# Routing in a two-layer expert model: token rows turned in half tiles, and late modulation blocks placed between other TensorE work

## What is computed

```
mod = silu(c) @ w_ada[l] + b_ada[l]            # shift1, scale1, gate1, shift2, scale2, gate2
h   = rms_norm(x, p['norm2']) * (1.0 + scale2) + shift2
x   = x + gate2 * expert_choice_ffn(h, ...)

def expert_choice_ffn(h, w_router, w1, w3, w2):
    cap = CAPACITY_FACTOR * n_tok // N_EXPERTS       # 64 latent, 16 context tokens each
    aff = jax.nn.softmax((xt @ w_router), axis=-1)   # 16 experts
    g, idx = lax.top_k(aff.T, cap)
    xe = xt[idx]
    hid = silu(xe @ w1) * (xe @ w3)
    ye = (hid @ w2) * g[..., None]
    out = zeros_like(xt).at[idx].add(ye)
```

## Time and profile before

| | us |
|---|---|
| median of 3 runs | 3060.97 |
| lowest, highest | 3060.78, 3061.44 |
| profiled execution | 3061.0 |
| its span in the trace | 3059.2 |
| layer 0, from the routing exponential to the first expert product | 854.91 to 909.18 |
| layer 1, the same | 2350.27 to 2395.15 |

### The profile page before, as it was taken

The page is one execution under the profiler, slowest core; times in us unless marked ns, Lnnn a source line. Parts: engine busy times, 40 slices in busy tenths (PEclk is TensorE's granted clock), DMA queues, the critical chain, the costliest instruction groups (busy, mean ns, idle before and its releaser), DMA issues.

```text
span 3059.2 us, 45356 instructions
## 1 busy us (share of the span) xinstructions
PE 2810.3 (92%) x16026; PEld 2211.3 (72%) x16026; DVE 2011.2 (66%) x3103; ACT 1648.0 (54%) x2425; POOL 265.4 (9%) x294
## 2 busy tenths in 40 slices
PE   6989989989979999999988898899998899999995
PEld 3868956979947777777657796588896677777774
DVE  3463356463459999999835524654645699999994
ACT  3263344253248777777634524432523677777774
POOL 0060012030010000000002300200201000000000
PEclk9999999999979999999999999999998899999997
DMA  7202100222369999999821021013043799999991
GB/s 292 69 22 92 59 29 28 84 72 97 114 248 353 338 337 337 337 336 337 310 72 63 29 95 57 1 56 127 29 145 119 255 335 338 339 336 338 333 346 70
DMA packets 280123, 564.13 MB, mean 184 GB/s; under 512 B 14040, under 2 KB 19872, under 8 KB 279328
## 3 DMA queue, kind: packets, MB, share of 16 engines
q1 hardware_dynamic: 273056, 543.25, 49.8%
q10 hardware_dynamic: 4448, 9.87, 0.9%
q0 software_dynamic: 2464, 8.91, 0.8%
HBM read 546.36 MB, written 15.63 MB: 184 GB/s over the span
## 4 chain that ended last, share of the span: by engine, by line
PE 66%; DVE 16%; ACT 7%; issue 5%; ACTq 2%; DVEq 1%; DMA 1%; POOL 1%; SPq 0%; POOLq 0%
PE mm L1033 23%; PE mm L1540 19%; DVE w_lo L2108 7%; PE mm L1056 6%; PE mm L1086 2%; DVE x L2116 2%; ACTq L2029 2%; DVE scratch L2335 1%; ACT w_hi L1618 1%; PE mm L1275 1%; ACT scratch L1618 1%; PE oo L990 1%; DVE scratch L2108 1%; PE mm L951 1%; ACT pt L1618 1%
## 5 line engine op out<-in xcount | busy, mean ns | idle before, releaser
L2108 DVE TENSOR_TENSOR w_lo<-ring,w_hi 128x1024 fp32r<-128x1024 f32 x768 | 911.8, 1219 | 86.3 <-ACT w_hi L1618 69.5
L1618 ACT ACTIVATE w_hi<-ring 128x1024 fp32r<-128x1024 f32 x768 | 803.4, 1059 | 277.6 <-PE mm L1540 255.4
L1033 PE MATMUL mm<-h_hi,ring_lo 128*128 128x320 f32 (+1 forms) x1344 | 313.6, 315 | 2.4 <-DVE h_lo L2108 2.0
L1033 PEld LDWEIGHTS mm<-h_hi,ring_lo 128*128 128x128 f32 (+1 forms) x1344 | 223.4, 188 | 16.4 <-issue 14.4
L1540 PE MATMUL mm<-w_lo,xa_hi 128*80 128x512 f32 x512 | 204.8, 400 | 18.2 <-DVE w_lo L2108 11.8
L2108 DVE TENSOR_TENSOR ring_lo<-ring,dw_hi 128x512 fp32r<-128x512 f32 (+1 forms) x104 | 70.1, 677 | 207.6 <-ACT dw_hi L1618 206.6
L1540 PE MATMUL mm<-w_lo,xb_hi 128*128 128x512 f32 x512 | 203.8, 398 | 0.0
L1540 PE MATMUL mm<-w_hi,xa_lo 128*80 128x512 f32 x512 | 202.7, 396 | 0.0
L1540 PE MATMUL mm<-w_hi,xa_hi 128*80 128x512 f32 x512 | 201.6, 394 | 0.0
L1540 PE MATMUL mm<-w_hi,xb_hi 128*128 128x512 f32 x512 | 199.8, 390 | 0.0
L1540 PE MATMUL mm<-w_hi,xb_lo 128*128 128x512 f32 x512 | 199.4, 389 | 0.0
(11 more groups left out here) (323 smaller groups left out, 6033.7 us busy)
## 6 DMA issues: line engine op xcount, KB each, us to landing
ring<-in_w_ff SPq DMA_DIRECT2D x384, 1024.0 KB, 6.2
ring<-in_w_ada SPq DMA_DIRECT2D x48, 1024.0 KB, 7.4
ring<-in_w_gate SPq DMA_DIRECT2D x24, 1024.0 KB, 6.2
ring<-in_w_in SPq DMA_DIRECT2D x16, 1024.0 KB, 9.6
ring<-in_w_o SPq DMA_DIRECT2D x8, 1024.0 KB, 7.9
x_spill<-x SPq DMA_DIRECT2D x2, 2560.0 KB, 13.2
ring<-in_w_br_da SPq DMA_DIRECT2D x4, 1024.0 KB, 5.1
ring<-in_w_br_mla SPq DMA_DIRECT2D x4, 1024.0 KB, 5.0
```

Of the source, the lines that this page charges most:

```text
L1033: last = pe.matmul(out[0:width, lo:hi], w_, h_[:, k, lo:hi], start=(k == 0 and i == 0), stop=(k == KT - 1 and i == 2))
L1618: return act.activation(out, in_, ACT.Copy, scale=scale)
L2108: return dve.tensor_tensor(out, in0, in1, op)
```

## The change

It has four parts.

1. The turns of h take half of `tp` (512 columns, one bank) each. There are ten in place of five. A half waits until the half two turns earlier has been read. ACT copies halves, and stores a tile after its second half.
2. The late blocks move on TensorE. Block 11 begins ahead of the logits' turn, block 12 behind it, and block 11 is turned ahead of the affinities' turn. In layer 0, block 15 begins behind the second token tile, where block 14 is turned, and block 15 is turned behind the fourth. ACT's copies move with them: block 11's stands before the exponential, behind the first shift.
3. POOL frees a block's chunks at other tiles: block 11 behind k = 2 (was k = 1), block 12 behind k = 4, block 13 behind k = 6 (was behind the last).
4. DVE writes `mod` behind `hot_p`, no more ahead of the positions' copy. `hotp_ready` now rises at `hot_p` already, so that `gather_p` no longer waits for `hotw_p`.

```diff
-    ... ("h_tok", TT), ...
+    ... ("h_tok", 2 * TT), ...
@@ POOL
-                    if k == 1:
+                    if k == 2:
                         ada_consumed(late[1:2])
                     if k == 4:
                         ada_consumed(late[2:3])
-                ada_consumed(late[3:])
+                    if k == 6:
+                        ada_consumed(late[3:4])
+                ada_consumed(late[4:])
@@ TensorE
                 ada_turn_late(l, late[0])
+                ada_begin(late[1], True)
                 pe.wait_ge(lgt_ready, l + 1)
...
-                ada_begin(late[1], True)
+                if len(late) > 2:
+                    ada_begin(late[2], True)
+                ada_turn_late(l, late[1])
                 pe.wait_ge(aff_ready, l + 1)
...
-                for n in late[2:]:
+                for n in late[3:5]:
                     ada_begin(n, True)
                     ada_turn_late(l, n - 1)
-                ada_turn_late(l, late[-1])
                 pe.wait_ge(h_ready, l * 2 * KT + 2 * KT)
                 for t in range(TT):
-                    wait_t_empty(pe, l, TR["h_tok"] + t)
-                    for k in range(KT):
-                        last = pe.transpose(tp[:, k * P:(k + 1) * P], h[:, k, t * P:(t + 1) * P], ident)
-                    last.then_inc(t_full, 1)
+                    for half in range(2):
+                        turn = TR["h_tok"] + 2 * t + half
+                        wait_t_empty(pe, l, turn if turn == TR["h_tok"] else turn - 1)
+                        for k in range(4 * half, 4 * half + 4):
+                            last = pe.transpose(tp[:, k * P:(k + 1) * P], h[:, k, t * P:(t + 1) * P], ident)
+                        last.then_inc(t_full, 1)
+                    if t == 1:
+                        for n in late[5:]:
+                            ada_begin(n, True)
+                            ada_turn_late(l, n - 1)
+                    if t == PRT - 1 and len(late) > 2:
+                        ada_turn_late(l, late[-1])
...
-                pe.wait_ge(hotp_ready, l + 1)
+                pe.wait_ge(hotp_ready, 2 * l + 1)
@@ ScalarE
                 ada_copy(late[0])
-                act.wait_ge(lg_ready, l + 1)
-                act.activation(aff[:, :, :], aff[:, :, :], ACT.Exp).then_inc(lg_e, 1)
-                ada_copy(late[1])
                 for k in range(KT):
                     shift_of(l, 1, k, [gain[:, 1, k, g:g + 1] for g in range(2)])
-                    if k % 2 and k // 2 < len(late) - 2:
-                        ada_copy(late[2 + k // 2])
+                    if k == 0:
+                        ada_copy(late[1])
+                        act.wait_ge(lg_ready, l + 1)
+                        act.activation(aff[:, :, :], aff[:, :, :], ACT.Exp).then_inc(lg_e, 1)
+                    if k in (1, 4, 6):
+                        for n in late[(k + 3) // 2:(k + 3) // 2 + 1]:
+                            ada_copy(n)
...
+                    if t == 1:
+                        for n in late[5:]:
+                            ada_copy(n)
```

More of the change, by code:

```diff
@@ L233 @@
     ("da_ctx", 1), ("da_new", 1), ("da", DA_N + TT), ("mla_ctx", 1), ("mla_new", 1),
-    ("mla", MLA_N), ("sw_ctx", 1), ("sw_vt", 1), ("sw_new", 1), ("sw", SW_PAIRS), ("raw", 1), ("lg_t", 1), ("aff", 1), ("h_tok", TT),
+    ("mla", MLA_N), ("sw_ctx", 1), ("sw_vt", 1), ("sw_new", 1), ("sw", SW_PAIRS), ("raw", 1), ("lg_t", 1), ("aff", 1), ("h_tok", 2 * TT),
     ("pos", 1), ("slots", 1), ("hot_p", 1), ("rows", 1), ("pairs", 0)])
@@ L1469, in _ @@
                 find_slots(TR["slots"], None, 0)
-                pe.wait_ge(hotp_ready, l + 1)
-                wait_t_read(pe, l, TR["h_tok"] + TT - 1)
+                pe.wait_ge(hotp_ready, 2 * l + 1)
+                wait_t_read(pe, l, TR["h_tok"] + 2 * TT - 1)
                 for g in range(2):
@@ L1480, in _ @@
                     last.then_inc(mm_full[j % 2], 1)
+                pe.wait_ge(hotp_ready, 2 * l + 2)
                 wait_t_empty(pe, l, TR["hot_p"])
@@ L1962, in _ @@
                 ada_copy(late[0])
-                act.wait_ge(lg_ready, l + 1)
-                act.activation(aff[:, :, :], aff[:, :, :], ACT.Exp).then_inc(lg_e, 1)
-                ada_copy(late[1])
                 for k in range(KT):
                     shift_of(l, 1, k, [gain[:, 1, k, g:g + 1] for g in range(2)])
-                    if k % 2 and k // 2 < len(late) - 2:
-                        ada_copy(late[2 + k // 2])
+                    if k == 0:
[5 more added lines that the diff above has]
+                            ada_copy(n)
                 for t in range(TT):
-                    wait_t_full(act, l, TR["h_tok"] + t)
-                    copy(tok[:, t, :], tp[:, :]).then_inc(t_empty, 1)
+                    for half in range(2):
+                        wait_t_full(act, l, TR["h_tok"] + 2 * t + half)
+                        last = copy(tok[:, t, 512 * half:512 * (half + 1)], tp[:, 512 * half:512 * (half + 1)])
+                        last.then_inc(t_empty, 1)
                     if t < LT:
@@ L2633, in _ @@
                 tt(cum_e[e16, :], cum_e[e16, :], mask_e[e16, :], ALU.mult).then_inc(pos_ready, 1)
[L2634 to L2645, removed]
                 wait_t_full(dve, l, TR["pos"])
@@ L2773, in _ @@
                 tt(hot_p, const[:, lo:lo + CAP_P].unsqueeze(1).to_broadcast([P, NE, CAP_P]),
-                   pos_t[:, PRT, :].unsqueeze(2).to_broadcast([P, NE, CAP_P]), ALU.is_equal)
+                   pos_t[:, PRT, :].unsqueeze(2).to_broadcast([P, NE, CAP_P]), ALU.is_equal).then_inc(hotp_ready, 1)
+                j = MM["late"]
+                wait_mm_full(dve, l, j)
+                dve.sem_inc(ada_turned, 1)
+                kept = [(40, ROWS["b_ada"][0] + 40, 8)] + [(0, ROWS["b_next"][0], 16)] * (l + 1 < DEPTH)
+                at = 0
+                for to, row, width in kept:
+                    tt(mod[:, to:to + width, :], mm[j % 2][:, 2 * at:2 * (at + width)].rearrange("p (m g) -> p m g", g=2),
+                       cols[:, row:row + width].unsqueeze(2).to_broadcast([P, width, 2]), ALU.add)\
+                        .then_inc(ada_done, width // 4)
+                    at += width
+                dve.drain()
+                dve.sem_inc(mm_empty[j % 2], 1)
                 slots(TR["slots"], None, 0)
```

## The result

| | kernel before | changed kernel |
|---|---|---|
| median time, us | 3061.22 | 3045.32 |
| lowest to highest of 5 runs | 3060.78 to 3061.58 | 3043.49 to 3046.37 |
| ratio, 95% interval | | 0.9947, 0.9932 to 0.9961 |
| profiled execution: time, span | 3061.0, 3059.2 | 3046.05, 3044.3 |

The kernel became 15.9 us faster. The forecast was 24.2 us, 3036.8; the result lies 1.3 us above its range.

A forecast was written before the change was run, and what follows sets the result against it. Bound in both routing stages: TensorE and ACT alternating on one `tp` for the turns of h, delaying the positions' turn. Layer 0 13.4 + 1.1, layer 1 8.6 + 1.1, together 24.2 us: 3036.8, range 3031 to 3044.

The forecast's parts named there:

- Block 11 ahead of the logits' turn: Layer 0: block 11's beginning moves into TensorE's 2.03 us wait, takes 1.92, and the logits' turn stays at 853.76.
- Start of the turns of h: Turns of h start at 865.9 in place of 877.12 in layer 0, at 2359.4 in layer 1.
- The halves: Turns of h in alternating halves: a tile costs 1.97 us at half clock, 1.65 at full clock.
- R: Start of the positions' turn: layer 0 from 892.60 to 879.2 (877.5 to 882), layer 1 from 2379.00 to 2370.4.
- `gather_p` behind `find_slots`: Behind R, both layers: `gather_p` starts when `find_slots` ends, no more 1.11 us later behind `hotw_p`.
- rows' turn in layer 1: Turn of the gathered rows at R + 10.6, before at R + 11.7; 1.1 us gained (0 to 1.3).
- Layer 1's R: Start of layer 1's positions' turn, with the positions ready last: 2370.4, 8.6 us earlier (6.8 to 9.0).
- Behind R in layer 0: Gathered rows turned at R + 11.4, before at R + 12.5; 1.1 us gained (0 to 2.1).
- the stores land late: Rival: layer 0's gather waits for the stores of h, leaves at 889; layer 0 gains 7.5, time 3044; chance 0.12.
- Outside the stages: Outside the stretches from first router to first expert product: 0 taken for the clock, 1.7 us either way per layer.
- experts swallow the gain: Rival: the time stays within 0.2%, some 6 us, of the kernel before; chance 0.05.
- the clock comes back: Rival: full clock from the first turn of h into the experts, 6.3 us more, span 3030.5; chance 0.11.

The follow-up runs named there:

- The pause: Changed kernel, with POOL waiting behind its third tile (k = 2) until DVE has copied the affinities into slot_of: 3039.99 us.
- the kernel with whole turns: Changed kernel with the turns of h in whole tiles again (part 1 undone, parts 2 to 4 kept): 3045.51 us.
- with pause, hold and spare matmuls: Changed kernel plus POOL's wait for DVE's affinity copies, SP holding expert chunks from the third until the first gather lands, and four plus six unread matmuls: 3028.91 us.

## Why the prediction was wrong in size

**Right.** *Block 11 ahead of the logits' turn* fits: 1.92 us, and the turn 16.38 behind the router's start in place of 16.35. *Start of the turns of h*: 12.78 behind the logits' turn, forecast 12.1; in layer 1 10.14, forecast 10.3. *The halves*: R in layer 0 came 13.9 us earlier, forecast 13.4, and block 15 among them cost 2.55, forecast 2.9. The clock rose within them, as the rival had it: the first two tiles took 1.88 each, the third 1.07. But the terms of the forecast's turns don't add up to its R: from 873.7 on, 3.5, 0.7, 1.3 to 1.97 and 0.69 give 879.9 to 880.6, not 878.5 to 880.0. By its own terms it had R 0.7 to 1.4 later than it took, and the clock's rise made that good; the close hit is in part luck. *`gather_p` behind `find_slots`* and *rows' turn in layer 1* (R + 10.62, forecast 10.6): right. *Additions into `mod`*: hidden.

**Layer 1's R, the first step that failed.** Forecast 8.6 us earlier, measured 5.8. The step took POOL's 4.21 us wait as lost time only and DVE's durations as fixed, "ready at 2351.4" less 1.5. It never asked what POOL would run beside once the wait was gone. That wait was also DVE's free way to the shared port. The pause shows it with 2.8 us, which is the whole of the miss.

**Behind R in layer 0, the second.** Forecast 1.1 us gained, measured 2.55 lost: 3.65 us. The rows' turn began 2.76 later than forecast and took 0.9 longer. Three things stand behind this. The gather left 0.95 later than "R + 5.2": the forecast saw the constant at R + 5.3 (measured R + 5.1) against the gather at R + 5.2 and called it a tie, but the constant's own issue of 0.76 and a wait of 0.30 stand on POOL's queue between them. The gather took 8.0 against "5.2 to 5.3", a duration read where the loads had drained. The 1.0 us that the forecast had left between landing and turn took up some of both. The rows' turn then ran at half clock, 1.97 against 1.06. The rival "the stores land late" had the mechanism and the place. It priced the gather's issue at 889 and kept 6 to 7 us for its landing; measured were 887.15 and 7.97. R + 14.16 in place of R + 11.4 is its smaller version, worth 2.8 and not 7.

**Outside the stages, the third.** Forecast 0, "1.7 us either way in each layer"; measured 2.2 us lost over two traces of each kernel. Of it 0.8 is in attention, inside that stretch's own spread. Of the 1.2 behind the stage of layer 0, 0.8 lie between the first and the last expert product, where two to four more slow products explain 0.4 to 0.8. The rest is no larger than the differences between two traces of one kernel.

Together: 24.2 less 2.8, 3.2 (3.65 less the 0.5 that R itself gave more) and 2.2 is 16.0, the difference of the mean spans; the medians show 15.9.

**The range** failed by 1.3 us. Its upper end, 3044, was that of one mishap, the stores. Two smaller ones and the spread together went past it. The case "experts swallow the gain" did not occur, nor "the clock comes back" as a whole: the clock came back in the turns of h, and was lost again at the 6 us wait for the rows, whose turn took 1.97 us.

## What to carry over

Before a wait is taken out of an engine, look at what its neighbours do in that time; here POOL's idle time was where DVE's small copies ran, and a pause of 1.5 us kept what its wait of 4.2 had given to DVE. A step that is brought forward meets other traffic: durations of DMAs that the sum rests on must be read where the queue will be as full as at the new place, and large loads without a deadline can be held for a few small transfers that have one. Where TensorE stands still just ahead of a long dense stretch, price the clock's return by the number of products that it slows and by their spacing at either clock. Compare single profiles by the stretches that the edit can touch, and then look whether the whole span follows: in the kernel with whole turns stages longer by 4.2 us left it where it was.

## What the runs showed of the hardware

- A DVE copy of 128x16 takes 0.17 us, or up to 1.53 beside POOL's two-input products of 1.54 each; a 128x80 product of two inputs 0.24 or 0.95. DVE's searches (16x512, one input, 0.68 us) lose nothing beside the same products.
- A gather of one pair's rows landed after 8.0 us beside the expert loads, all transfers together at 390 to 403 GB/s, and after 5.2 to 5.3 with them held; the four stores after 6.0 to 7.8 against 2.6 to 5.2. The Trainium skill, "DMA: Bandwidth & Descriptors", Issuing engines are not separate DMA queues, has all transfers interleave on the same engines; the trace agrees in that no store had to wait for the queue to drain (the last had landed by 886.1, and the DMA share was 1.04 until 896), at a price of some 3 us each.
- Ten matmuls in each layer that compute nothing of use, in time that TensorE stood idle, came with a kernel 6.5 us faster (3038.85 in place of 3045.32). Some 4.4 of it lie in the experts, whose first products then ran at the granted clock's upper level, 2.4 GHz: 2 and 0 slow ones in place of 10 and 13. A slow start costs 0.2 us for each 512-column product that runs at the lower level.
- Just ahead of the logits' turn, beside one of POOL's products, a DVE instruction of 16x128 took 1.54 to 1.57 us where one of 16x512 took 0.47, and the product took 1.78 in place of 1.54. So POOL seems to lose time there too; no run tests it.
- The fastest kernel, with pause, hold and spare matmuls, takes 3028.91 us, 16 us under the changed kernel and 33 under the kernel before as measured beside it (3061.96). The change's own parts brought half of that.
